# Second output projection as seven block products instead of eight, in a two-layer float32 transformer kernel on one Trainium2 core

## The chip, the cores and the metric

The kernel runs on one core of a Trainium2 chip. The metric is the device time of one execution in microseconds (us), as the median of three runs. TensorE (PE in the profile) multiplies, VectorE (DVE), ScalarE (ACT) and GpSimd (POOL) do the elementwise work, and SyncE (SP) issues most DMAs. Only VectorE and ScalarE read the PSUM banks that TensorE writes; GpSimd works in SBUF alone.

## The reference

Two transformer layers over a sequence of 512 tokens with model width 1024, all in float32. The first is an attention layer; the second is what matters here:

```
h = rms_norm(x, norm_mix);  proj = h @ w_in
a = nsa_attention(...) @ w_branch_attn        # 512 x 1024
b = pool_mixer(...) @ w_branch_pool           # 512 x 1024
ga, gb = split(sigmoid(g_merge))
x = x + (ga * a + gb * b) @ w_out             # the second output projection, 512 x 1024 by 1024 x 1024
h = rms_norm(x, norm_mlp)
x = x + square(relu(h @ w_ff1)) @ w_ff2       # feed forward, width 4096
return rms_norm(x, norm_final)
```

## The kernel before

Every matrix product is made from three: each operand is split into a high part (a copy by ScalarE into the type fp32r) and a low part (raw minus high, by VectorE or GpSimd), and `three` issues high x high, high x low and low x high into one PSUM bank. The program is one fixed instruction order per engine, written by hand, with counting semaphores between the engines; each engine takes its instructions strictly in that order.

Around the change the work runs so. In the branch stage TensorE makes 16 products of 12 matmuls each, in the order `BRANCH` (for column block e = 0 to 7 one for the pooled branch, n = 1, and one for attention, n = 0), round four banks. `branch_product` for e waits for `br_lo_done`, counted by `branch_low(e)` on VectorE, and for `r_free`, counted by `gate` of the product four earlier. VectorE multiplies each product with its gate (`gate`, L2610, one input in PSUM), adds the two (L2645, counted by `mix_done`, here called mix e), makes the low part of the branch weights two blocks ahead (`branch_low(e + 2)`, L2153), the low part of a unit of 1024 columns of the projection's weights (`w2o_lo`, L2652) and of the mixed activations (`m_lo`, L2655). ScalarE makes the high parts. GpSimd has nothing to do from 594.9 us, when its last attention work (`add_turned`) ends, to 690.8 us.

The second projection is `residual(R, ready2, product2, h3)`: for each of four row tiles i and two column halves n, eight chunks k of three matmuls with 512 columns. VectorE adds each bank to x (`add_x`, L2178, counted by `r_free`); when a row tile has both halves, ScalarE squares and sums it (`squares`), takes the root, and VectorE scales it (`norm`, L2111 and L2114). TensorE turns the normed tile (`h_transposes`, h3, L1015, eight 128 x 128 transposes) in the middle of the next tile's products, and VectorE and ScalarE make its high and low part (`take_halves`, L2166 and L2171, with `input_high` on ScalarE between). The first two feed-forward column tiles (`ff_tile`) are then made for the first three row tiles (384 columns), the last set of transposes between them, and then for the last row tile (128 columns):

```
for c in range(2):
    ff_tile(c, 0, 3 * P)
    if c == 0:
        h3(3)
pe.wait_ge(h_lo_done, halves("h3", NT - 1, 1) + 1)
for c in range(2):
    ff_tile(c, 3 * P, S).then_inc(a_full, 1)
```

The weights of the projection (`w2o0`, `w2o1`, one column half each) come by two DMAs issued before the branch stage. The first halves of w_ff1 (`f1_half`) are loaded by SyncE after the last branch product (two) and after the last use of `w2o0` (two); after `w2o1` follow the pairs of w_ff2. Behind the last h3 tile GpSimd makes sums of w_ff2 blocks (`pair_sums`), since the last product of the kernel already works with seven block products.

## Time and profile before

| | |
|---|---|
| median of 3 runs | 1022.66 us (1022.52 to 1022.76) |
| the profiled execution: its own time | 1021.85 us |
| its span, from the first to the last instruction | 1019.8 us |
| PE busy | 1006.5 us (99%) |
| VectorE busy | 680.1 us (67%) |
| ScalarE busy | 555.3 us (54%) |
| GpSimd busy | 418.7 us (41%) |
| granted TensorE clock | 1.00 over the span |

Times in the views are us from the span's start. In the windows' rows stand the stretch, its length, then for PE, PE's weight loads, VectorE, ScalarE and GpSimd the busy us with the number of instructions, the mean granted TensorE clock (1.00 is full), the DMA share and GB/s. In the timelines stand start, duration, engine, line, operation, output and inputs, shapes, how many instructions the row merges, and in brackets the idle time ahead of it with what ended it. Durations of matmuls overlap, so TensorE's rate is read from the starts.

### The profile page before, as it was taken

What the parts mean: (1) busy time and instruction counts of PE and PEld (TensorE: products, weight loads), DVE (VectorE), ACT (ScalarE), POOL (GpSimd) and SP (SyncE); (2) the same over time, 40 slices, a digit from 0 to 9 for tenths busy, and PEclk for the clock granted to TensorE, in tenths of its full rate; (3) what the DMA queues carried; (4) which work ended last, traced back from release to release, by engine and by line L of the source; (5) the groups of instructions that cost most, each with busy time, mean ns of one, the idle gap of its engine ahead of it and who ended that gap; (6) DMA issues with size and microseconds to landing.
All of it is one profiled execution on the core that took longest, in us unless ns stands there. A gap on an engine that the chain in (4) does not pass through costs nothing.

```text
span 1019.8 us, 14243 instructions
## 1 busy us (share of the span) xinstructions
PE 1006.5 (99%) x5158; PEld 828.2 (81%) x5158; DVE 680.1 (67%) x1201; ACT 555.3 (54%) x1013; POOL 418.7 (41%) x403
## 2 busy tenths in 40 slices
PE   9999999999999999999999999999999999999997
PEld 7788877778778898878887788888888888888886
DVE  5578898788984256733577889344222325999997
ACT  8455354777862456544667874224443446554555
POOL 0024012666720003900354520007769865875563
PEclk9999999999999999999999999999999999999999
DMA  9533321337140384132200453249999951443552
GB/s 339 105 98 97 100 62 42 84 84 196 53 175 1 123 284 129 45 100 63 63 2 1 149 166 100 83 136 308 353 343 333 340 208 62 155 137 143 207 186 83
DMA packets 100165, 146.24 MB, mean 143 GB/s; under 512 B 6480, under 2 KB 60496, under 8 KB 100096
## 3 DMA queue, kind: packets, MB, share of 16 engines
q1 hardware_dynamic: 86800, 130.75, 39.5%
q10 hardware_dynamic: 12768, 12.88, 4.1%
q0 software_dynamic: 528, 1.70, 0.9%
q8 instruction: 41, 0.67, 0.3%
q14 instruction: 28, 0.23, 0.1%
HBM read 123.69 MB, written 21.63 MB: 142 GB/s over the span
## 4 chain that ended last, share of the span: by engine, by line
PE 89%; DVE 6%; ACT 3%; issue 2%; POOL 0%; ACTq 0%; DVEq 0%; POOLq 0%
PE bank L966 60%; PE bank L1478 5%; PE bank L1479 5%; PE bank L1480 5%; PE bank L1358 2%; PE bank L1148 2%; PE bank L1367 2%; PE bank L1119 1%; DVE x L2244 1%; PE bank L1381 1%; DVE stats L2243 1%; DVE u_lo L2146 1%; PE bank L1132 1%; PE bank L1268 1%; PE bank L1015 1%
## 5 line engine op out<-in xcount | busy, mean ns | idle before, releaser
L2661 DVE TENSOR_TENSOR w_lo<-wring,w_hi 128x1024 fp32r<-128x1024 f32 x32 | 50.9, 1589 | 108.0 <-ACT w_hi L1999 108.0
L2146 DVE TENSOR_TENSOR u_lo<-wring,u_hi 128x1024 fp32r<-128x1024 f32 (+2 forms) x69 | 83.3, 1215 | 52.1 <-ACT u_hi L1652 51.6
L966 PE MATMUL bank<-u_hi,h_hi 128*128 128x512 f32 (+1 forms) x288 | 110.9, 385 | 0.1
L966 PE MATMUL bank<-u_hi,h_lo 128*128 128x512 f32 (+1 forms) x288 | 109.3, 379 | 0.0
L966 PE MATMUL bank<-u_lo,h_hi 128*128 128x512 f32 (+1 forms) x288 | 109.0, 378 | 0.0
L1652 ACT ACTIVATE u_hi<-wring 128x1024 fp32r<-128x1024 f32 (+1 forms) x64 | 66.0, 1033 | 69.3 <-PE bank L966 55.1
L966 PE MATMUL bank<-h_hi,w_hi 128*128 128x512 f32 (+2 forms) x272 | 103.2, 379 | 0.0
L966 PE MATMUL bank<-h_hi,w_lo 128*128 128x512 f32 (+2 forms) x272 | 103.1, 379 | 0.0
L966 PE MATMUL bank<-h_lo,w_hi 128*128 128x512 f32 (+2 forms) x272 | 103.1, 379 | 0.0
L966 PE MATMUL bank<-h_hi,u_hi 128*128 128x512 f32 x224 | 93.4, 417 | 0.4 <-ACT arena L1594 0.2
L966 PE MATMUL bank<-h_hi,u_lo 128*128 128x512 f32 x224 | 87.7, 392 | 0.0
L966 PE MATMUL bank<-h_lo,u_hi 128*128 128x512 f32 x224 | 87.6, 391 | 0.0
L1478 PE MATMUL bank<-s_hi,f_hi 128*128 128x512 f32 x224 | 87.3, 390 | 0.0
L1479 PE MATMUL bank<-s_hi,f_lo 128*128 128x512 f32 x224 | 87.2, 389 | 0.0
L1480 PE MATMUL bank<-s_lo,f_hi 128*128 128x512 f32 x224 | 87.2, 389 | 0.0
L1999 ACT ACTIVATE w_hi<-wring 128x1024 fp32r<-128x1024 f32 x32 | 33.9, 1060 | 91.9 <-PE bank L966 91.9
L2894 POOL TENSOR_SCALAR arena<-arena,stats 128x128 f32<-128x128 f32 (+3 forms) x64 | 40.6, 645 | 94.9 <-DVE stats L2617 94.8
L2687 DVE TENSOR_TENSOR s_lo<-wring,s_hi 128x2048 fp32r<-128x2048 f32 (+1 forms) x32 | 67.8, 2119 | 5.6 <-ACT s_hi L2029 5.6
L2840 POOL TENSOR_SCALAR x<-x,stats 128x128 f32<-128x128 f32 (+3 forms) x64 | 47.8, 753 | 55.4 <-DVE stats L2353 55.4
L966 PEld LDWEIGHTS bank<-u_hi,h_hi 128*128 128x128 f32 x288 | 54.1, 188 | 11.6 <-issue 1.2
L966 PEld LDWEIGHTS bank<-u_lo,h_hi 128*128 128x128 f32 x288 | 54.1, 188 | 10.3
L2029 ACT ACTIVATE s_hi<-wring 128x2048 fp32r<-128x2048 f32 (+1 forms) x32 | 54.3, 1696 | 14.0 <-PE bank L1480 13.8
(401 smaller groups left out, 2596.2 us busy)
## 6 DMA issues: line engine op xcount, KB each, us to landing
wring<-in_w_in SPq DMA_DIRECT2D x60, 512.0 KB, 3.9
wring<-in_w_ff ACTq DMA_DIRECT2D x12, 1024.0 KB, 9.4
wring<-sums_kept SPq DMA_DIRECT2D x16, 768.0 KB, 4.2
wring<-in_w_ff SPq DMA_DIRECT2D x22, 512.0 KB, 6.7
wring<-in_w_ff SPq DMA_DIRECT2D x32, 256.0 KB, 3.2
sums_kept<-wring SPq DMA_DIRECT2D x22, 256.0 KB, 4.9
wring<-in_w_out SPq DMA_DIRECT2D x2, 2048.0 KB, 12.7
wring<-in_w_ff SPq DMA_DIRECT2D x4, 1024.0 KB, 6.8
```

The costliest lines, as they stand in the source:

```text
L966: last = mm(b, lhs, rhs, start=(start and n == 0), stop=(stop and n == 2))
L1478: mm(b, f[0][:, token], w[0][:, high], start=start, stop=False)
L1479: mm(b, f[1][:, token], w[0][:, high], start=False, stop=False)
L1480: return mm(b, f[0][:, token], w[1][:, lows], start=False, stop=stop)
L1652: run(u_hi[hi_place(u)][:, 0:unit_cols(u)], raw_unit(u), ACT.Copy).then_inc(u_hi_done, 1)
L1999: run(dst, src, ACT.Copy).then_inc(w_hi_done, 1)
L2029: run(s_hi[m % 4][:, 0:PAIR - at], pair_raw(m)[:, at:PAIR], ACT.Copy).then_inc(s_hi_done, 1)
L2146: done = v.tensor_tensor(u_lo[raw_place(u)][:, cols], raw_unit(u)[:, cols], u_hi[hi_place(u)][:, cols].bitcast(F32), ALU.subtract)
L2661: v.tensor_tensor(cut(w_lo[ring3(m)]), src, cut(w_hi[ring3(m)]).bitcast(F32), ALU.subtract).then_inc(w_lo_done, 1)
L2687: v.tensor_tensor(s_lo[pair_place(m)][:, at:PAIR], pair_raw(m)[:, at:PAIR], s_hi[m % 4][:, 0:PAIR - at].bitcast(F32), ALU.subtract)
L2840: g.tensor_scalar(logits1[u % 8], logits1[u % 8], den[:, u:u + 1], unit_factor, ALU.mult, ALU.mult).then_inc(scaled, 1)
L2894: g.tensor_scalar(place, place, den2[:, u:u + 1], gates[:, i, at:at + 1], ALU.mult, ALU.mult).then_inc(scaled, 1)
```

## The change

The projection is cut into halves in all three dimensions: weights into quarters B11, B12, B21, B22 (512 x 512), activations into quarters of 256 tokens by 512. Eight block products become seven (B11, T2, T1, B22, B21, T3, T4 in this order, the list `seven`), with sums of weight quarters (T1 to T4) and of activation quarters (S1, S2, S4, and a difference in place in the lower half of m chunks 0 to 3). Each product is two row tiles t of four chunks. GpSimd makes the weight sums, three of 2048 columns per partition and one in two halves of 1024 (`quarter_sums`); VectorE the activation sums (`side_work`, three instructions of 256 columns for each of four chunks, and `last_side`, 1024 columns) and the low parts of quarters (`quarter_low`, two of 1024 columns each) and sides (`side_low`). Some of the fourteen results belong in two places of x; a running copy of B11 and T2, later with T3, in SBUF (`running`) is added to x by GpSimd, 512 columns six times (`add_running`). ScalarE makes the high parts of all of them and the first running copy. The h3 transposes move behind T3 (two sets) and into the first feed-forward tile (two sets), and the first two feed-forward tiles are made in halves of 256 columns. The unit high and low parts 0 and 1 of w_ff1 move ahead of the squares, and four buffers move. The loads of w_ff1 and w_ff2 wait for B21 and T3 in place of the projection's last products.

```diff
+        seven = ("B11", "T2", "T1", "B22", "B21", "T3", "T4")
...
+        HIGHS = ("B11", "B22", "T1", "T2", "B21", "T3", "T4")
+        QUARTER_SUM_ORDER = ("T1", "T3", "T2", "T4")
+        QUARTER_READ_BY = {"B11": "T1", "T1": "T2", "B22": "T2", "T2": "T4", "B21": "T4"}
+        high_count = lambda name, h: 2 * HIGHS.index(name) + h + 1
+        low_count = lambda name, h: 2 * seven.index(name) + h + 1
...
+        out2_bank = {"B11": 2, "T2": 6, "T1": 0, "B22": 4, "B21": 2, "T3": 6, "T4": 6}
+        def out2_used(name):
+            return R_OUT2 + 2 * seven.index(name) + 2
+        def out2_added(i):
+            return R_OUT2 + (2 * seven.index("B21") + i if i < 2 else 2 * seven.index("T4") + i - 2) + 1
...
+            out2_sides = {"B11": (m_hi[0:4], m_lo[0:4], 0), "B21": (m_hi[4:8], m_lo[4:8], 0), "T3": (m_hi[0:4], m_lo[0:4], 2 * P),
+                          "T4": (m_hi[4:8], m_lo[4:8], 2 * P), "T2": "S2", "T1": "S1", "B22": "S4"}
+            out2_behind = {"B11": R_OUT2 - 1, "B21": out2_used("T2") - 1, "T3": out2_used("T2") - 1, "T4": out2_used("T3") - 1}
+            def out2(name, t):
+                if name in out2_behind:
+                    pe.wait_ge(r_free, out2_behind[name] + t)
+                q = seven.index(name)
+                for j in range(4):
+                    if t == 0 and j % 2 == 0:
+                        pe.wait_ge(w2o_lo_done, low_count(name, j // 2))
+                    if isinstance(out2_sides[name], str):
+                        if t == 0 and j == 0:
+                            pe.wait_ge(side_lows, SIDE_LOWS + ("S2", "S1", "S4").index(out2_sides[name]) + 1)
+                        side = side_hi[out2_sides[name]], side_lo[out2_sides[name]]
+                        rows = slice((2 * j + t) * P, (2 * j + t + 1) * P)
+                    else:
+                        highs, lows, at = out2_sides[name]
+                        if t == 0 and name in ("B11", "B21"):
+                            pe.wait_ge(m_lo_done, (0 if name == "B11" else 4) + j + 1)
+                        side = highs[j], lows[j]
+                        rows = slice(at + t * P, at + (t + 1) * P)
+                    last = three(bank[out2_bank[name] + t][:, :], (w2o_hi[q % 4], w2o_lo[name, j // 2]), slice(512 * j, 512 * (j + 1)), side, rows,
+                                 False, j == 0, j == 3, j % 2 * 512)
+                last.then_inc(r_full, 1)
...
-            residual(R, ready2, product2, h3)
-            R += 2 * NT
-            def ff_tile(c, first, end):
-                for k in range(KC):
+            def ff_tile(c, first, end, chunks=range(KC)):
+                for k in chunks:
                     last = three(bank[AT[("ff", c)] % 2][:, first:end], (w_hi[ring3(c)], w_lo[ring3(c)]), slice(k * P, (k + 1) * P),
                                  (h_hi, h3_lo), slice(k * S + first, k * S + end), True, k == 0, k == KC - 1)
                 return last
...
+            for name in seven:
+                for t in range(2):
+                    out2(name, t)
+                    if name == "T3":
+                        h3(t)
+            pe.wait_ge(r_free, out2_used("B21"))
+            pe.wait_ge(h_lo_done, halves("h3", 1, 1) + 1)
+            a_bank(("ff", 0))
+            pe.wait_ge(w_lo_done, 1)
+            ff_tile(0, 0, 2 * P, range(3))
+            h3(2)
+            ff_tile(0, 0, 2 * P, range(3, KC))
+            h3(3)
+            a_bank(("ff", 1))
+            pe.wait_ge(w_lo_done, 2)
+            ff_tile(1, 0, 2 * P)
             pe.wait_ge(h_lo_done, halves("h3", NT - 1, 1) + 1)
             for c in range(2):
-                ff_tile(c, 3 * P, S).then_inc(a_full, 1)
-            pe.wait_ge(r_free, R)
+                ff_tile(c, 2 * P, S).then_inc(a_full, 1)
+            pe.wait_ge(r_free, out2_added(NT - 1))
...
+            def quarter_high(name, h):
+                q = seven.index(name)
+                if name == "B11":
+                    arrived(act, "w2o0")
+                elif name == "B22":
+                    arrived(act, "w2o1")
+                elif name in QUARTER_SUM_ORDER:
+                    act.wait_ge(quarter_sums, QUARTER_SUMS + QUARTER_SUM_ORDER.index(name) + 1)
+                if q >= 4:
+                    act.wait_ge(r_full, out2_used(seven[q - 4]))
+                run(w2o_hi[q % 4][:, D * h:D * (h + 1)], w2o_raw[name, h], ACT.Copy).then_inc(w2o_hi_done, 1)
+            def side_high(name):
+                act.wait_ge(r_full, R_OUT2)
+                act.wait_ge(side_sums, SIDE_SUMS + (13 if name == "S4" else 12))
+                run(side_hi[name][:, :], side_raw[name], ACT.Copy).then_inc(side_highs, 1)
+            EARLY_HIGHS = [(name, h) for name in HIGHS[0:4] for h in range(2)]
             for e in range(KC):
-                n, c = e // 4, slice(UNIT * (e % 4), UNIT * (e % 4 + 1))
-                if e % 4 == 0:
-                    arrived(act, f"w2o{n}")
-                run(w2o_hi[n][:, c], wring[:, SLOT * n:SLOT * (n + 1)][:, c], ACT.Copy).then_inc(w2o_hi_done, 1)
+                quarter_high(*EARLY_HIGHS[e])
                 if 1 <= e < KC - 2:
                     branch_high(e + 2)
-                act.wait_ge(mix_done, e + 1)
-                run(m_hi[e][:, :], gaT[:, e, :], ACT.Copy).then_inc(m_hi_done, 1)
+                if e >= 4:
+                    act.wait_ge(mix_done, e + 1)
+                    run(m_hi[e][:, :], gaT[:, e, :], ACT.Copy).then_inc(m_hi_done, 1)
+                    act.wait_ge(side_sums, SIDE_SUMS + 3 * (e - 4) + 2)
+                    run(m_hi[e - 4][:, :], gaT[:, e - 4, :], ACT.Copy).then_inc(m_hi_done, 1)
+            def copy_first(t):
+                act.wait_ge(r_free, R_OUT2 + t + 1)
+                run(running[t], bank[out2_bank["B11"] + t][:, :], ACT.Copy).then_inc(first_copied, 1)
+            side_high("S2")
+            side_high("S1")
+            copy_first(0)
+            side_high("S4")
+            copy_first(1)
+            for name in ("B21", "T3", "T4"):
+                for h in range(2):
+                    quarter_high(name, h)
...
-            for i in range(NT):
-                if i >= 1:
-                    input_high("h3", i - 1)
-                squares(2 * NT, R_OUT2, i)
-                if i in (1, 2):
-                    unit_hi(i - 1)
-            input_high("h3", NT - 1)
+            unit_hi(0)
+            unit_hi(1)
+            nc.scalar.preload_act_table(ACT.Sqrt)
+            for i in range(2):
+                squares(2 * NT, out2_added(i), i)
+            for i in range(2):
+                input_high("h3", i)
+            for i in range(2, NT):
+                squares(2 * NT, out2_added(i), i)
             unit_hi(2)
...
+            def quarter_low(name, h):
+                dve.wait_ge(w2o_hi_done, high_count(name, h))
+                if name in QUARTER_READ_BY:
+                    dve.wait_ge(quarter_sums, QUARTER_SUMS + QUARTER_SUM_ORDER.index(QUARTER_READ_BY[name]) + 1)
+                q = seven.index(name)
+                v.tensor_tensor(w2o_lo[name, h][:, :], w2o_raw[name, h], w2o_hi[q % 4][:, D * h:D * (h + 1)].bitcast(F32), ALU.subtract)\
+                    .then_inc(w2o_lo_done, 1)
+            def mixed2_low(k):
+                dve.wait_ge(m_hi_done, 2 * k + 2 if k < 4 else 2 * k - 7)
+                dve.wait_ge(side_sums, SIDE_SUMS + (3 * k + 3 if k < 4 else 13))
+                v.tensor_tensor(m_lo[k][:, :], gaT[:, k, :], m_hi[k][:, :].bitcast(F32), ALU.subtract).then_inc(m_lo_done, 1)
+            def side_work(j):
+                upper, lower, other = gaT[:, j, 0:2 * P], gaT[:, j, 2 * P:S], gaT[:, j + 4, 2 * P:S]
+                s1, s2 = side_part(side_raw["S1"], j), side_part(side_raw["S2"], j)
+                dve.wait_ge(mix_done, j + 5)
+                v.tensor_tensor(s1, lower, other, ALU.add).then_inc(side_sums, 1)
+                v.tensor_tensor(lower, upper, lower, ALU.subtract).then_inc(side_sums, 1)
+                dve.wait_ge(side_sums, SIDE_SUMS + 3 * j + 1)
+                v.tensor_tensor(s2, s1, upper, ALU.subtract).then_inc(side_sums, 1)
+                mixed2_low(j)
+            def last_side():
+                dve.wait_ge(r_full, R_OUT2)
+                dve.wait_ge(side_sums, SIDE_SUMS + 12)
+                by_chunk = lambda a: a.rearrange("p (j s) -> p j s", j=4)
+                v.tensor_tensor(by_chunk(side_raw["S4"]), gaT[:, 4:8, 0:2 * P], by_chunk(side_raw["S2"]), ALU.subtract).then_inc(side_sums, 1)
+            def side_low(n, name):
+                dve.wait_ge(side_highs, SIDE_HIGHS + n + 1)
+                if name == "S2":
+                    dve.wait_ge(side_sums, SIDE_SUMS + 13)
+                v.tensor_tensor(side_lo[name][:, :], side_raw[name], side_hi[name][:, :].bitcast(F32), ALU.subtract).then_inc(side_lows, 1)
+            def out2_add(name, t):
+                part = bank[out2_bank[name] + t][:, :]
+                dve.wait_ge(r_full, R_OUT2 + 2 * seven.index(name) + t + 1)
+                xs = lambda i, n: x[:, i, n * 512:(n + 1) * 512]
+                if name == "T2":
+                    dve.wait_ge(first_copied, FIRST_COPIED + t + 1)
+                elif name == "T3":
+                    dve.wait_ge(running_added, RUNNING_ADDED + t + 1)
+                elif name == "T1":
+                    v.tensor_tensor(xs(2 + t, 1), xs(2 + t, 1), part, ALU.add)
+                    dve.wait_ge(running_added, RUNNING_ADDED + t + 1)
+                elif name == "B22":
+                    dve.wait_ge(r_free, out2_used("T1") - 1 + t)
+                elif name == "B21":
+                    dve.wait_ge(r_free, out2_used("B11") - 1 + t)
+                elif name == "T4":
+                    dve.wait_ge(running_added, RUNNING_ADDED + 2 * t + 3)
+                place = {"B11": xs(t, 0), "T2": running[t], "T1": xs(t, 1), "B22": xs(t, 1), "B21": xs(t, 0), "T3": running[t], "T4": xs(2 + t, 0)}[name]
+                v.tensor_tensor(place, place, part, ALU.add).then_inc(r_free, 1)
+            LOW_AT = {3: (("B11", 0), ("B11", 1)), 6: (("T2", 0),), 7: (("T2", 1), ("T1", 0))}
...
-                n, c = e // 4, slice(UNIT * (e % 4), UNIT * (e % 4 + 1))
-                dve.wait_ge(w2o_hi_done, e + 1)
-                v.tensor_tensor(w2o_lo[n][:, c], wring[:, SLOT * n:SLOT * (n + 1)][:, c], w2o_hi[n][:, c].bitcast(F32), ALU.subtract)\
-                    .then_inc(w2o_lo_done, 1)
-                dve.wait_ge(m_hi_done, e + 1)
-                v.tensor_tensor(m_lo[e][:, :], gaT[:, e, :], m_hi[e][:, :].bitcast(F32), ALU.subtract).then_inc(m_lo_done, 1)
+                if e >= 4:
+                    side_work(e - 4)
+                for name, h in LOW_AT.get(e, ()):
+                    quarter_low(name, h)
...
+            last_side()
+            side_low(0, "S2")
             dve.wait_ge(x_back, 16 * NT)
...
+            out2_add("B11", 0)
+            side_low(1, "S1")
+            quarter_low("T1", 1)
+            out2_add("B11", 1)
+            quarter_low("B22", 0)
+            quarter_low("B22", 1)
+            out2_add("T2", 0)
+            side_low(2, "S4")
+            mixed2_low(4)
+            out2_add("T2", 1)
+            mixed2_low(5)
+            mixed2_low(6)
+            out2_add("T1", 0)
+            mixed2_low(7)
+            quarter_low("B21", 0)
+            out2_add("T1", 1)
+            quarter_low("B21", 1)
+            quarter_low("T3", 0)
+            out2_add("B22", 0)
+            quarter_low("T3", 1)
+            quarter_low("T4", 0)
+            out2_add("B22", 1)
+            quarter_low("T4", 1)
+            unit_lo(0)
+            out2_add("B21", 0)
+            unit_lo(1)
+            out2_add("B21", 1)
+            norm(2 * NT, 0, xn3)
+            norm(2 * NT, 1, xn3)
+            out2_add("T3", 0)
+            take_halves("h3", 0, V_G3, h3_lo)
+            out2_add("T3", 1)
+            take_halves("h3", 1, V_G3, h3_lo)
+            out2_add("T4", 0)
+            norm(2 * NT, 2, xn3)
+            out2_add("T4", 1)
+            take_halves("h3", 2, V_G3, h3_lo)
+            norm(2 * NT, 3, xn3)
+            take_halves("h3", 3, V_G3, h3_lo)
...
+            raw_quarter = lambda n, h: wring[:, SLOT * n + QUARTER * h:SLOT * n + QUARTER * (h + 1)]
+            t1_raw, t2_raw = (region_of[place][:, at:at + QUARTER] for place, at in (quarter_at["T1"], quarter_at["T2"]))
+            arrived(pool, "w2o0")
+            arrived(pool, "w2o1")
+            pool.wait_ge(last_lo_done, 2)
+            g.tensor_tensor(t1_raw, raw_quarter(1, 0), raw_quarter(0, 0), ALU.subtract).then_inc(quarter_sums, 1)
+            g.tensor_tensor(raw_quarter(1, 0), raw_quarter(1, 1), raw_quarter(1, 0), ALU.subtract).then_inc(quarter_sums, 1)
+            pool.wait_ge(mix_done, 4)
+            pool.wait_ge(quarter_sums, QUARTER_SUMS + 1)
+            g.tensor_tensor(t2_raw, raw_quarter(1, 1), t1_raw, ALU.subtract).then_inc(quarter_sums, 1)
+            pool.wait_ge(quarter_sums, QUARTER_SUMS + 3)
+            for h in range(2):
+                part = slice(D * h, D * (h + 1))
+                done = g.tensor_tensor(w2o_raw["T4", h], raw_quarter(0, 1)[:, part], t2_raw[:, part], ALU.subtract)
+            done.then_inc(quarter_sums, 1)
+            def add_running(i, n, t):
+                xs = x[:, i, n * 512:(n + 1) * 512]
+                g.tensor_tensor(xs, xs, running[t], ALU.add).then_inc(running_added, 1)
+            pool.wait_ge(x_back, 16 * NT)
+            for t in range(2):
+                pool.wait_ge(r_free, out2_used("T2") - 1 + t)
+                add_running(t, 1, t)
+            for t in range(2):
+                pool.wait_ge(r_free, out2_used("T3") - 1 + t)
+                add_running(2 + t, 0, t)
+                add_running(2 + t, 1, t)
```

## Rows read from the trace of the kernel before

**Rows 1.** The page, part 1: busy time and share of the span of each engine.
```profile
PE 1006.5 (99%) x5158; PEld 828.2 (81%) x5158; DVE 680.1 (67%) x1201; ACT 555.3 (54%) x1013; POOL 418.7 (41%) x403
```

**Rows 2.** Windows: branch stage, then second projection.
```profile
602.50:636.94 34.44, 34.44 (x153) 28.52 (x152) 31.62 (x41) 16.17 (x19) 0.00 (x0) 1.00 0.45 138
636.94:683.17 46.23, 46.23 (x217) 38.52 (x216) 20.61 (x31) 11.85 (x19) 0.00 (x0) 1.00 0.25 80
```

**Rows 3.** Timeline of PE: start, duration, line, operation, shapes.
```profile
634.22 0.39 PE L966 MATMUL bank<-a_hi,br_hi 128*128 128x512 f32 x1
...
636.94 0.39 PE L966 MATMUL bank<-w2o_hi,m_hi 128*128 128x512 f32 x1
...
683.17 0.33 PE L966 MATMUL bank<-h_hi,w_hi 128*128 128x384 f32 x1
...
687.36 1.03 PE L1015 MATMUL bank<-consts,arena 128*128 128x128 f32 x8
...
688.15 0.42 PE L966 MATMUL bank<-h_hi,w_hi 128*128 128x384 f32 x1
...
692.41 0.22 PE L966 MATMUL bank<-h_hi,w_hi 128*128 128x128 f32 x1
...
697.71 0.45 PE L966 MATMUL bank<-h_hi,w_hi 128*128 128x512 f32 x1
```

**Rows 4.** Timeline of PE, matmuls of 256 columns, four starts apart.
```profile
593.69 0.28 PE L1381 MATMUL bank<-pt_hi,v_both 128*128 128x256 f32 x1
...
594.16 0.28 PE L1381 MATMUL bank<-pt_hi,v_both 128*128 128x256 f32 x1
```

**Rows 5.** Timeline of VectorE at the head of the branch stage.
```profile
600.97 0.42 DVE L2589 TENSOR_TENSOR a_lo<-arena,a_hi 128x256 fp32r<-128x256 f32 x1 [0.48 <-ACT a_hi L1927]
601.31 1.22 DVE L2153 TENSOR_TENSOR br_lo<-wring,br_hi 128x1024 fp32r<-128x1024 f32 x1
602.45 1.38 DVE L2610 TENSOR_TENSOR arena<-arena,bank 128x512 f32<-128x512 f32 x2
603.86 0.69 DVE L2645 TENSOR_TENSOR arena<-arena 128x512 f32<-128x512 f32 x1
...
605.61 0.68 DVE L2655 TENSOR_TENSOR m_lo<-arena,m_hi 128x512 fp32r<-128x512 f32 x1
606.21 0.68 DVE L2610 TENSOR_TENSOR arena<-arena,bank 128x512 f32<-128x512 f32 x1
```

**Rows 6.** Timeline of GpSimd, adds and subtractions with two inputs in SBUF.
```profile
271.47 0.74 POOL L2822 TENSOR_TENSOR junk<-arena,x 128x256 f32<-128x256 f32 x1
...
585.22 1.31 POOL L2905 TENSOR_TENSOR br_lo<-wring,br_hi 128x512 fp32r<-128x512 f32 x1
...
690.83 1.29 POOL L2919 TENSOR_TENSOR wring<-wring 128x512 f32<-128x512 f32 x1 [95.94 <-DVE h_lo L2171]
692.08 2.26 POOL L2920 TENSOR_TENSOR wring<-wring 128x512 f32<-128x512 f32 x1
...
883.11 2.49 POOL L2938 TENSOR_TENSOR arena<-arena 128x256 f32<-128x256 f32 x1 [1.20 <-PE bank L1480]
```

**Rows 7.** Timeline of VectorE at the same moments.
```profile
585.68 0.69 DVE L2599 CUSTOM_DVE_ANT_0 arena<-bank,consts 128x512 f32<-128x512 f32 x1 [0.25 <-PE bank L1358]
...
691.00 2.20 DVE L2661 TENSOR_TENSOR w_lo<-wring,w_hi 128x1024 fp32r<-128x1024 f32 x1 [0.25 <-ACT w_hi L1999]
...
882.72 2.28 DVE L2687 TENSOR_TENSOR s_lo<-wring,s_hi 128x2048 fp32r<-128x2048 f32 x1
```

**Rows 8.** Timeline of VectorE, from a bank add to the norm behind it.
```profile
659.79 0.69 DVE L2178 TENSOR_TENSOR x<-x,bank 128x512 f32<-128x512 f32 x1 [3.05 <-PE bank L966]
...
662.09 0.16 DVE L2111 RECIPROCAL stats<-stats 128x1 f32<-128x1 f32 x1 [1.60 <-ACT stats L1539]
662.28 0.76 DVE L2114 TENSOR_SCALAR arena<-x,stats 128x1024 f32<-128x1024 f32 x1
```

**Rows 9.** Windows: behind the last matmul.
```profile
1014.00:1019.80 5.80, 0.00 (x0) 0.00 (x0) 1.55 (x3) 1.97 (x5) 0.00 (x0) 0.94 0.66 248
```

More of the change, by code:

```diff
@@ L499, in wo_high_of @@
             return zb_half[:, k:k + count, :] if k < 4 else qk1_half[:, 1, (k - 4) // 2:(k - 4) // 2 + 1, (K_LO, OUTS)[k % 2], :]
[L501 to L504 removed]
+        QUARTER, SIDE = SLOT // 2, D
@@ L1856, in _ @@
             high(U2)
[L1857 removed]
+            squares(NT, 2, 0)
             for u in range(1, HI_UNITS - 1):
```

107 lines of the change are left out of this document (58 added, 49 removed).

## The prediction

> **What bounds the kernel now.** The page comes first: PE is busy 99% of the span [rows 1]. TensorE sets the time, so a change is worth the PE time it removes minus the PE idle time it makes. The windows cut the place into the branch stage and the second output projection; PE idles in neither, and VectorE is busy 31.6 of 34.4 us in the first and 20.6 of 46.2 us in the second [rows 2]. The reader should note that VectorE is nearly full just where GpSimd is about to get work. The PE timeline gives the pitches and the marks: the last branch product starts at 634.22 and the projection at 636.94, so a matmul of 512 columns has a pitch of 2.72 / 12 = 0.227 us; the first feed-forward tiles run from 683.17 to 697.71 [rows 3].
>
> **What is removed.** The projection has 4 row tiles x 2 column halves x 8 chunks x 3 = 192 matmuls, and seven products have 7 x 2 row tiles x 4 chunks x 3 = 168: 24 x 0.227 = 5.4 us. The first feed-forward tiles now cost 4.19 + 4.26 us at 384 columns and 5.30 us at 128, 13.75 us without the transposes [rows 3]. At 256 columns the pitch is (594.16 - 593.69) / 4 = 0.1175 us [rows 4], so 96 of them take 11.3 us, 2.5 us less. Gross gain 7.9 us; the stretch from 636.94 to 697.71 (60.8 us) would be 52.9 us if PE never waited.
>
> **Durations.** VectorE, both inputs in SBUF: 0.34 us from start to start at 256 columns, 0.60 at 512, 1.14 at 1024; with one input in PSUM 0.60 at 512 [rows 5]. GpSimd, two inputs: 0.74 us at 256 and 1.29 at 512 [rows 6]. No row has 2048 columns. A straight line through these two gives 4.6 us, four times 1.29 gives 5.2; I take 4.6 and keep 5.2 for the range. For 1024 it is 2.4 us.
>
> **How the two engines share.** The view to read is the timelines of GpSimd and VectorE side by side. The 1024 subtraction at 691.00 finds the GpSimd add of 690.83 running: it takes 2.20 us in place of 1.22, which is waiting to about 692.1 and then its own time; and the add of 692.08 takes 2.26 in place of 1.29, having waited for that subtraction. At 883.11 a 256 add takes 2.49 us behind the 2048 subtraction of 882.72, which ends at 885.0. An operation with a PSUM input is not held (585.68, 0.69 us inside the add of 585.22) [rows 6, 7]. So whole instructions exclude each other, the waiting engine goes next, and I take it that a 4.6 us add shuts VectorE out for 4.6 us. The row for such a length is VectorE's (2.2 us), not GpSimd's. The Trainium skill (SBUF — State Buffer, on the shared GPSIMD/Vector port) has the same rule: an exclusive lock held for the full instruction, not a split of bandwidth; it speaks against this change, and the rows agree with it up to 2.2 us. The skill (GPSIMD Engine Reference, section 3.1) gives 4.5 us for a 2048 float32 add; by that the sum below would be about 0.3 us lower.
>
> **Branch stage, step by step.** The last of the sixteen products (p = 15) starts at 634.22 [rows 3], so product p starts at 634.22 - 2.72 (15 - p). Product 2e needs branch_low(e), which VectorE issues behind mix(e - 2); a product also needs the gate of four earlier. GpSimd's first sum is ready when last_low(1) ends (601.4), waits for the branch_low of 601.31 and runs 602.5 to 607.1. Gates 1 and 2 (PSUM) pass; mix 0, issued at 603.86 now [rows 5], waits to 607.1. The second sum takes the port at 607.7, when mix 0 ends, to 612.2. Gate 3 passes; mix 1 runs 612.2 to 612.8, branch_low(3) to 614.0. Product 6, due at 609.74, starts at 614.1: PE waits 4.4 us. Without sums VectorE catches up until mix 3 (621.1) and branch_low(5) (622.2). The third sum holds the port 622.2 to 626.8, the low part of B11,0 follows to 627.9, then the fourth sum in two halves with B11,1 between them to 633.75; mix 4 ends at 634.35, branch_low(6) at 635.5. Product 12, after the first shift due at 630.4, starts at 635.6: 5.2 us more. These two waits come from the length of one GpSimd instruction; sums of 5.2 us make them 12 us together. From there VectorE keeps pace and the last branch product ends at 646.5, 9.6 us late.
>
> **Between the stages.** Before, m_lo of chunk 7 was due 5 us into the first product. Now B11's fourth chunk is due after 2.0 us (9 matmuls), and stands behind gate 15, mix 7, three side operations of 256 columns, ScalarE's high part and a low part, on VectorE also behind the low part of T2,0. From mix 6 on that is worked out as 651.5 against 648.5: 3.0 us. T2 then waits for the low parts T2,1 and T1,0, the 1024 side S4 and the low part of S2, 4 x 1.14 us, while PE has 3.4 us of B11 left: 1.2 us. T2 starts at 656.1.
>
> **Inside the projection.** From T2's start VectorE has, up to B21's second add: two side, nine quarter and two unit low parts of 1024 columns (13 x 1.14), four m_lo and twelve bank adds (16 x 0.60), 24.4 us, and two running adds of GpSimd that shut it out for 1.3 us each. By this queue B21,0 is added at 25.2 us, though PE had it at 19.0. From an add to the reciprocal of its norm pass 2.30 us [rows 8], and norm 0 is ready at 27.9; PE, done with T3,0 at 24.5, waits for it: 3.4 us. Four more running adds fall on the low parts of take_halves 0 and 1, and the feed-forward start waits 0.5 us for h_lo. norm 2 (add of T4,0 at 39.0, plus the squares) is ready at 41.6 when PE wants it at 39.5: 2.1 us. norm 3 stands behind take_halves 2; from the start of a set of transposes to the last low part behind it are 691.00 - 0.25 - 687.36 = 3.4 us [rows 3, 7], then 0.95 us for reciprocal and norm [rows 8]: PE waits 1.8 us at the last transposes. The stretch from T2's start to the end of the first tiles takes 47.7 + 7.8 = 55.5 us.
>
> **What I cost at nothing.** ScalarE's added copies (four running and side highs, m_hi, quarters): it is busy 16.2 of 34.4 and 11.9 of 46.2 us [rows 2]. GpSimd's own time: it is idle in both stretches, and its weight sums of the next stage start after the last h_lo as before. The DMAs of w_ff1 wait for B21 and T3 in place of the end of the projection, earlier relative to it; if they were late, unit_hi(4) would be next. The Sqrt table load moves ahead of the squares.
>
> **Sum.** Waits 4.4 + 5.2 + 3.0 + 1.2 + 7.8 = 21.6 us against 7.9 us: +13.7 us, on the profiled execution's 1021.85 us (span 1019.8) 1035.6; the median of the runs shown is 0.8 us above that execution, so 1036.4 us.
>
> **Rivals.** (a) Long sums don't hold the port throughout, short ones do: branch_low(3) and (6) come in time, 9.6 us fall away, +4 us, 1027. For it: no row shows a GpSimd hold beyond 1.3 us. Against it: those of 1.3 us are undivided. (b) The port costs nothing here at all: VectorE's queue alone is left, waits 2.5 + 1.2 between the stages and 2.9 inside, 6.6 against 7.9: -1.3 us, 1021.4. Against it stands 691.00. (c) Faster: VectorE's queue is not late inside and between the stages (operations overlap more than my pitches, or ready marks come earlier) and the sums fall into its gaps: only the removed matmuls count, up to -7.9, 1014.8. It decides once all waits together are under 5.8 us; the stage before was 92% full on VectorE, which speaks against it. (d) The clock falls in the long waits. The only fall in this trace is behind the last matmul, with PE idle from 1014 on: a mean of 0.94 over 5.8 us is a level of one half for the last 0.7 us, so it fell after some 5 us of idling [rows 9], and the second wait is 5.2 us. One product at 1.2 GHz in place of 2.4 costs 2.7 us: +3 to +6 on top, 1040 to 1043. The Trainium skill (TensorE: Matmul & The Clock Gate, HAM oscillation) says that an idle gap of this order halves the clock; by that the time would be 1040.
>
> **Chances.** The forecast with (d) as its upper part, +9 to +20: 0.65 (0.5 without a clock fall, 0.15 with). (a), +2 to +9: 0.16. (b): 0.09. (c): 0.08. Above 1043: 0.02. 0.2% is 2.0 us, about what a measurement of this kernel tells from no change. Faster 0.09, same 0.09, slower 0.82. Range 1025 to 1043: its lower end is (a) less 2 us, its upper one the sums of 5.2 us (+2.4) or two clock falls.
>
> **What would show it.** Right: the GpSimd rows of the sums near 4.6 us; mix 0 and mix 1 on VectorE of 4 to 5 us; PE idle ahead of products 6 and 12, 4 to 5 us each; PE idle ahead of B11's fourth chunk and of three sets of h3 transposes; VectorE without gaps from B11 to B21. Wrong: PE busy 34.4 us over the branch stage (then (a) or (b)), or VectorE waiting for PE inside the projection (then (c)); a granted clock under 1.00 beside these waits is (d).

## The result, and the profile after

The changed kernel takes 1042.43 us (median of 4 runs, 1040.19 to 1042.70) against 1022.67 (4 runs, 1022.52 to 1022.76) for the kernel before: ratio 1.0187, 95% interval 1.0171 to 1.0203. The forecast was 1036.4 in a range of 1025 to 1043. The page of the kernel after, its busy times and the rows of its 40 slices for PE, VectorE, GpSimd and the granted clock, then the shares of the chain:

```profile
span 1040.9 us, 14292 instructions
PE 1009.3 (97%) x5134; PEld 827.9 (80%) x5134; DVE 716.8 (69%) x1231; ACT 565.3 (54%) x1024; POOL 451.4 (43%) x414
PE   9999999999999999999999988888999999999997
DVE  5578997789984349435577878984222325999997
POOL 0024012667610006500554544126669974875553
PEclk9999999999999999999999988999999999999999
PE 81%; DVE 11%; ACT 4%; issue 3%; POOL 0%; ACTq 0%; DVEq 0%; POOLq 0%
```

PE was 99% busy [rows 1]; it now has five slices with gaps, and they are the slices from the branch products to the first feed-forward tiles. The same view by windows, the branch stage to the start of block B11 and from there to the first full feed-forward tile, answers to [rows 2]:

```profile
602.50:651.43 48.93, 40.57 (x153) 32.38 (x152) 40.47 (x40) 14.49 (x18) 21.51 (x5) 0.86 0.32 97
651.43:718.79 67.36, 57.55 (x298) 48.91 (x296) 56.37 (x71) 28.51 (x41) 17.39 (x11) 0.95 0.39 129
```

The reader should see three things. Both stretches grew: 34.4 to 48.9, and 60.8 to 67.4 though fewer matmuls stand in it. VectorE is busy 56.4 us of the second. And the granted clock is under 1 in both (0.86, 0.95), where it was 1.00. The PE timeline shows each wait as the idle time in brackets, with what ended it:

```profile
613.68 0.80 PE L1016 MATMUL bank<-pm_hi,br_hi 128*128 128x512 f32 x1 [3.81 <-DVE br_lo L2264]
...
637.65 0.80 PE L1016 MATMUL bank<-pm_hi,br_hi 128*128 128x512 f32 x1 [4.54 <-DVE br_lo L2264]
...
656.36 0.50 PE L1016 MATMUL bank<-w2o_hi,m_hi 128*128 128x512 f32 x1 [2.73 <-DVE m_lo L2766]
...
688.50 1.09 PE L1065 MATMUL bank<-consts,arena 128*128 128x128 f32 x8 [2.25 <-DVE arena L2225]
...
701.90 1.09 PE L1065 MATMUL bank<-consts,arena 128*128 128x128 f32 x8 [1.79 <-DVE arena L2225]
...
707.71 1.35 PE L1065 MATMUL bank<-consts,arena 128*128 128x128 f32 x8 [2.93 <-DVE arena L2225]
```

These are product 6, product 12, B11's fourth chunk, and the transposes of input tiles 0, 2 and 3. GpSimd and VectorE side by side in the branch stage:

```profile
601.52 5.44 POOL L3112 TENSOR_TENSOR arena<-wring 128x2048 f32<-128x2048 f32 x1 [6.67 <-DVE a_lo L2701]
606.92 5.02 POOL L3113 TENSOR_TENSOR wring<-wring 128x2048 f32<-128x2048 f32 x1
623.75 5.53 POOL L3116 TENSOR_TENSOR arena<-wring,arena 128x2048 f32<-128x2048 f32 x1 [11.82 <-DVE arena L2814]
```

```profile
603.83 3.68 DVE L2814 TENSOR_TENSOR arena<-arena 128x512 f32<-128x512 f32 x1
607.43 0.67 DVE L2722 TENSOR_TENSOR arena<-arena,bank 128x512 f32<-128x512 f32 x1
608.14 4.35 DVE L2814 TENSOR_TENSOR arena<-arena 128x512 f32<-128x512 f32 x1
612.41 1.21 DVE L2264 TENSOR_TENSOR br_lo<-wring,br_hi 128x1024 fp32r<-128x1024 f32 x1
...
625.59 8.11 DVE L2760 TENSOR_TENSOR w2o_lo_B<-wring,w2o_hi 128x1024 fp32r<-128x1024 f32 x2
```

Mixings 0 and 1 take 3.68 and 4.35 us in place of 0.69; the gate between them reads PSUM and is not held, also inside a GpSimd sum. Behind mixing 1 stands branch_low(3), which product 6 needs. Last, the windows of the granted clock (the number before the last two) around product 6:

```profile
612.00:614.00 2.00, 0.32 (x1) 0.32 (x2) 2.00 (x3) 1.07 (x2) 0.00 (x0) 0.71 1.06 320
614.00:616.00 2.00, 2.00 (x6) 1.52 (x6) 1.97 (x4) 1.98 (x2) 0.00 (x0) 0.50 0.29 119
616.00:618.00 2.00, 2.00 (x6) 1.62 (x5) 0.68 (x1) 0.02 (x1) 0.00 (x0) 0.50 0.00 0
618.00:620.00 2.00, 2.00 (x7) 1.53 (x7) 0.69 (x1) 0.00 (x0) 0.00 (x0) 0.59 0.00 0
620.00:625.00 5.00, 5.00 (x23) 4.12 (x22) 2.53 (x4) 0.00 (x0) 1.25 (x1) 1.00 0.30 84
```

The clock drops to 0.50 (1.2 GHz of 2.4) in the wait and product 6 then runs 5.29 us instead of 2.72.

### The profile page after: what moved, and what is told of

Its sections match the earlier page's. It is cut to its first block, busy times and chain, and to the rows that moved or that the text cites. A ratio compares the mean times of both kernels' runs of the same rounds, so it can differ in the third digit from the quotient of the medians.

```text
span 1040.9 us, 14292 instructions
## 1 busy us (share of the span) xinstructions
PE 1009.3 (97%) x5134; PEld 827.9 (80%) x5134; DVE 716.8 (69%) x1231; ACT 565.3 (54%) x1024; POOL 451.4 (43%) x414
## 4 chain that ended last, share of the span: by engine, by line
PE 81%; DVE 11%; ACT 4%; issue 3%; POOL 0%; ACTq 0%; DVEq 0%; POOLq 0%
PE bank L1016 52%; PE bank L1550 5%; PE bank L1552 5%; PE bank L1551 5%; PE bank L1408 2%; PE bank L1198 2%; PE bank L1417 2%; PE bank L1169 1%; DVE x L2356 1%; PE bank L1431 1%; DVE stats L2355 1%; DVE u_lo L2257 1%; PE bank L1182 1%; DVE w2o_lo_B L2760 1%; DVE w2o_lo_T L2760 1%
## 5 line engine op out<-in xcount | busy, mean ns | idle before, releaser
L1016 PE MATMUL bank<-h_hi,w_hi 128*128 128x512 f32 (+1 forms) x272 | 103.4, 380 | 0.1
L1016 PE MATMUL bank<-h_lo,w_hi 128*128 128x512 f32 (+1 forms) x272 | 103.0, 379 | 0.0
L1016 PE MATMUL bank<-h_hi,w_lo 128*128 128x512 f32 (+1 forms) x272 | 102.9, 378 | 0.0
L2140 ACT ACTIVATE s_hi<-wring 128x2048 fp32r<-128x2048 f32 (+1 forms) x32 | 54.3, 1696 | 13.8 <-PE bank L1552 13.6
```

Source lines behind the costliest of these rows:

```text
L1016: last = mm(b, lhs, rhs, start=(start and n == 0), stop=(stop and n == 2))
L2140: run(s_hi[m % 4][:, 0:PAIR - at], pair_raw(m)[:, at:PAIR], ACT.Copy).then_inc(s_hi_done, 1)
```

## The experiments

Two stretches on the PE timeline give a common measure for all of them: A, from the last 256-column matmul ahead of the branch stage (near 597) to B11's first matmul (in kernels without blocks, the projection's first), and B, from there to the first full feed-forward tile. Read so, the change made A 14.5 us longer (39.9 to 54.5) and B 6.6 us (60.8 to 67.4, against the 52.9 that the prediction gives for no wait).

| kernel | A, us | B, us | time, us | ratio to before (95%) |
|---|---|---|---|---|
| before | 39.9 | 60.8 | 1022.5 to 1022.9 | |
| after | 54.5 | 67.4 | 1042.43 | 1.0187 (1.0171 to 1.0203) |
| e1: sums in pieces of 512 | 45.1 | 68.4 | 1032.33 | 1.0089 (1.0072 to 1.0107) |
| e2: no sums | 40.1 | 65.8 | 1027.58 | 1.0046 (1.0031 to 1.0061) |
| e3: filler matmuls | 50.6 | 67.4 | 1038.28 | 1.0148 (1.0132 to 1.0164) |
| e4: before + halves | 40.0 | 59.3 | 1020.98 | 0.9982 (0.9973 to 0.9991) |
| e5: order behind B22 | 52.3 | 63.0 | 1037.20 | 1.0151 (1.0135 to 1.0166)|
| e6: pieces, all orders | 43.1 | 64.8 | 1028.92 | 1.0063 (1.0050 to 1.0076) |
| e7: sums on VectorE | 41.5 | 69.2 | 1031.31 | 1.0083 (1.0069 to 1.0097) |
| e8: before + two long sums | 48.2 | 60.8 | 1030.95 | 1.0084 (1.0069 to 1.0099) |
| e9: e7 with orders | 40.8 | 65.9 | 1027.96 | 1.0054 (1.0039 to 1.0069) |
| e10: orders, no sums | 40.0 | 64.1 | 1025.56 | 1.0028 (1.0017 to 1.0039) |

**e1, the sums in pieces.**

```
+def weight_quarter_sum(out, left, right, columns=QUARTER, piece=512):
+    for at in range(0, columns, piece): ... g.tensor_tensor(out[:, part], left[:, part], right[:, part], ...)
-g.tensor_tensor(t1_raw, raw_quarter(1, 0), raw_quarter(0, 0), ALU.subtract)
+weight_quarter_sum(t1_raw, raw_quarter(1, 0), raw_quarter(0, 0))     # the same for the others
```

> The changed kernel with each weight sum cut into pieces of 512 columns (16 GpSimd instructions in place of 5), nothing left out. Theory (the length of one GpSimd instruction is what delays branch_low): no wait of VectorE for the port is longer than 1.3 us, the wait ahead of product 6 falls from 4.0 us to under 1, the one ahead of product 12 from 4.7 to 1 to 3 us because about 10 us of exclusion are still laid on a full VectorE, and neither wait brings the clock down: 1029 to 1034 us. Rival (it is the amount of GpSimd work, not its length): both waits stay about as long, 1039 to 1043 us.

Measured 1032.33. Not one column less is added, and the time falls by 10.1 us: most of what the sums cost is the length of one instruction. VectorE's instructions of the branch stage take 13.8 us more than their own time beside the long sums and 9.8 us more beside the pieces, so both engines still pay. GpSimd's first two sums and VectorE's first instructions beside them:

```profile
601.29 6.79 POOL L3115 TENSOR_TENSOR arena<-wring 128x512 f32<-128x512 f32 x4 [6.67 <-DVE a_lo L2701]
608.04 7.47 POOL L3115 TENSOR_TENSOR wring<-wring 128x512 f32<-128x512 f32 x4
```

```profile
603.59 1.62 DVE L2814 TENSOR_TENSOR arena<-arena 128x512 f32<-128x512 f32 x1
605.14 0.67 DVE L2722 TENSOR_TENSOR arena<-arena,bank 128x512 f32<-128x512 f32 x1
605.84 1.07 DVE L2814 TENSOR_TENSOR arena<-arena 128x512 f32<-128x512 f32 x1
```

The mixings now take 1.62 and 1.07 us, a piece 1.7 to 1.9 instead of 1.29 [rows 6]: the engines take turns. Product 6 no longer waits; product 12 still waits 2.7 us, and there the expectation failed: the clock fell behind that wait too, to 0.50 for 3.4 us, and twice more at the transposes of tiles 0 and 3.

**e2, no sums.** The weight sums are left out: GpSimd memsets of the same places stand for them, so the weights of T1 to T4 are constants and the output is not the reference's.

```
-g.tensor_tensor(t1_raw, raw_quarter(1, 0), raw_quarter(0, 0), ALU.subtract).then_inc(quarter_sums, 1)
+g.memset(t1_raw, 1.0).then_inc(quarter_sums, 1)        # the same for the others
```

> The changed kernel with the weight sums left out: GpSimd fills their places with memsets, which write SBUF and read nothing, so the second projection is computed with wrong weights. Theory: the waits ahead of products 6 and 12 and the two falls of the clock behind them are gone, 8.7 + 5.8 us, of which 1 to 2 come back as the wait ahead of T2 that the slow clock had hidden: 1029 to 1031 us. What is left over the kernel before is VectorE's queue in the projection. Rival (VectorE's own added work delays branch_low): still a wait of some us ahead of product 12, over 1034 us. If a memset excludes VectorE as a sum does, its rows are shorter (2 us) and so are VectorE's waits.

Measured 1027.58, 1.4 us under the expected stretch and still slower than before. A is back at 40.1: the whole lateness of the branch stage, clock included, was the sums'. Without them the kernel is 14.9 us faster than the changed one: the 10.1 us of their length (e1) and 4.8 us of their amount. B is 65.8, 13 us over its waitless 52.9. T2's wait for its low parts, hidden in the changed kernel, shows here with 1.1 us. One row pair surprised:

```profile
604.13 1.82 POOL L3113 MEMSET wring<- 128x2048 f32 x1
```

```profile
604.73 0.69 DVE L2814 TENSOR_TENSOR arena<-arena 128x512 f32<-128x512 f32 x1
```

The mixing runs inside a memset of 2048 columns and takes its normal 0.69 us: this GpSimd instruction, which only writes, does not hold VectorE. The later memsets show the same: a low part of 1024 columns takes its 1.22 us beside them.

**e3, filler matmuls for the clock.**

```
 e, n = BRANCH[at]
+if at in (6, 12):
+    pe.wait_ge(r_free, 2 * NT + at - 3)
+    for _ in range(12):
+        mm(bank[6][:, :], a_hi[:, 0:P], a_hi[:, 0:S], start=True, stop=True)     # read by nobody
 pe.wait_ge(br_lo_done, e + 2)
```

> The changed kernel with 12 added matmuls of 512 columns into an unused bank ahead of the waits of products 6 and 12 each; they fill 2.7 us of waits of 4.0 and 4.7 us and change no result. Theory (the clock falls because PE idles, and costs on top of the waits): no fall at these two places, the products behind take 2.7 us in place of 5.3 and 3.1, 1036 to 1038 us, since 1 us may come back ahead of T2. Rival (the time behind the waits is VectorE's, the slow products are hidden by it): 1041 to 1043 us.

Measured 1038.28, 4.15 us less than after, just above the theory's stretch. Twelve matmuls are 2.7 us of work; they shortened the idle time at product 6 to 1.15 us and the clock stayed at 1.00 there. At product 12 1.87 us were left and the clock still fell (0.66 over 635 to 640), against the expectation. Added work on the waiting engine made the kernel faster: the slow clock is a cost of its own.

**e4, the halves alone, on the kernel before.**

```
-    ff_tile(c, 0, 3 * P)
+    ff_tile(c, 0, 2 * P)
...
-    ff_tile(c, 3 * P, S).then_inc(a_full, 1)
+    ff_tile(c, 2 * P, S).then_inc(a_full, 1)
```

> The kernel before with one part alone: the first two feed-forward tiles in halves of 256 columns instead of 384 and 128, the last transposes between them. 96 matmuls of 0.1175 us in place of 13.75 us: 2.5 us less on PE. The first half tile is 1.4 us shorter than the tile of 384 columns, so the last transposes come 1.4 us earlier and wait for norm 3 by 0.1 to 0.8 us, and the last low parts may come 0.5 us late. Theory: 1.2 to 2.4 us faster, 1020.3 to 1021.5 us. Rival (the earlier transposes wait as long as the halves save): 1022 to 1023 us.

Measured 1020.98, faster than before, and the only kernel of this study that is. On its PE timeline, 24 matmuls run from 684.00 to the transposes, 72 after them (the first full tile starts at 697.06):

```profile
684.00 0.28 PE L966 MATMUL bank<-h_hi,w_hi 128*128 128x256 f32 x1
...
687.50 1.09 PE L1015 MATMUL bank<-consts,arena 128*128 128x128 f32 x8 [0.47 <-DVE arena L2114]
688.35 0.36 PE L966 MATMUL bank<-h_hi,w_hi 128*128 128x256 f32 x1
```

Without the wait of 0.47 that is 3.0 + 8.7 = 11.7 us against 13.75: the halves give 2.0 us, and a new wait of half a microsecond: counted from the projection's first matmul, TensorE is ready for the transposes of tile 3 after 49.3 us in place of 50.4, and they start after 49.7.

**e5, the order of two queues.**

```
-quarter_low("T4", 1); unit_lo(0); out2_add("B21", 0); unit_lo(1); out2_add("B21", 1)
-norm(2 * NT, 0, xn3); norm(2 * NT, 1, xn3)
+out2_add("B21", 0); quarter_low("T4", 1); norm(2 * NT, 0, xn3)
+out2_add("B21", 1); unit_lo(0); norm(2 * NT, 1, xn3); unit_lo(1)
...
-take_halves("h3", 2, V_G3, h3_lo); norm(2 * NT, 3, xn3)
+take_halves("h3", 2, V_G3, h3_lo, between=norm 3)      # and ScalarE: unit_hi(2) behind input_high("h3", 2)
```

> The changed kernel, long sums and all, with one thing altered: the order of VectorE's and ScalarE's queues behind product B22. The adds of B21 and norms 0 and 1 stand ahead of the last T4 low and of the two feed-forward lows, norm 3 stands between the products and the lows of input transpose 2, and ScalarE's high of the third feed-forward tile goes behind input high 2. Theory (the waits ahead of the transposes of tiles 0 and 3 are queueing: VectorE had work of later use in front of the adds and the norms): the waits of 2.4 and 3.2 us fall under 0.6 us each, and the fall of the clock behind the second, 1.6 us, goes with them, so the time falls by 4 to 7 us, to 1035 to 1038.5. Rival (the waits are the chain itself, from the last matmul over add, squares, root and norm to the transpose): the time moves by less than 1 us, 1041.5 to 1042.5.

Measured 1037.20, 5.2 us less. The 2.3 us ahead of the transposes of tile 0 are gone, those of tile 3 wait 0.26 in place of 2.93, and the clock no longer falls there. So both were queueing. What came instead is 1.24 us at the second row tile of T4 (its bank is free only after T3's second add, which stands behind the low parts of input 0) and 0.7 at the first feed-forward matmul; tile 2's 1.8 us stayed, being the chain of add, squares, root and norm itself.

**e6, pieces and all orders together.** e1 and e5, and:

```
-LOW_AT = {3: (("B11", 0), ("B11", 1)), 6: (("T2", 0),), 7: (("T2", 1), ("T1", 0))}
+LOW_AT = {5: (("B11", 0), ("B11", 1)), 6: (("T2", 0),)}        # T2,1 behind side_low S2, T1,0 behind side_low S1
+for chunks in (range(3), range(3, 4)):                          # TensorE: B11 by chunks, both row tiles
+    for t in range(2):
+        out2("B11", t, chunks)
-ff_tile(0, 0, 2 * P, range(3))
+ff_tile(0, 0, 2 * P, range(5))
```

> The kernel with the sums in pieces of 512 columns (1032.3 us) with the order of the run beside it, and with four more moves: the lows of block B11 behind mixing 5 instead of 3, the lows of T2's second half and of T1 behind the low of side sum S2, the products of B11's first three chunks for both row tiles ahead of the fourth chunk of either, and the transposes of tile 2 behind five chunks of the first feed-forward tile instead of three. Theory (what is left over the gross gain is queueing in front of five waits, and the clock that falls in them): of the 12.6 us of waits in the pieces' trace 9 to 11 go (2.7 ahead of product 12, 2.2 of 3.8 around B11 and T2, 5 of 5.9 at the norms) and about 3 us of slow clock, so 1018.5 to 1022.5, on a par with the kernel before or faster. Rival (the waits move to other places, since VectorE is full while GpSimd adds): 1026 to 1031.

Measured 1028.92: the theory's 1018.5 to 1022.5 was wrong, and the rival right. The clock stays at 1.00 from the branch stage on, but instead of e1's seven waits there are thirteen, 10.9 us in all, none over 1.6 us, and all but one ended by VectorE. The waits moved. A short wait also costs more than its idle time: in e2, B11's ninth matmul starts at 639.75 and the next at 642.86, which is 0.15 us more than the pitch of 0.23 and the idle 2.73, and the two starts behind it come 0.12 us late; about 0.27 us for each restart. The other waits between matmuls of 512 columns in e6, e9 and e10 show the same 0.24 to 0.29 us, where the idle time is half a microsecond or more.

**e7, the sums on VectorE**, T1's behind mixing 0, T3's behind 2, T2's behind 3 and T4's halves behind 4 and 5:

```
+def weight_sum(at): ... v.tensor_tensor(t1_raw, raw_quarter(1, 0), raw_quarter(0, 0), ALU.subtract).then_inc(quarter_sums, 1) ...
+    weight_sum(e)                        # in VectorE's loop over the mixings; GpSimd's five sums taken out
```

> The changed kernel with the five weight sums on VectorE, behind mixings 0, 2, 3, 4 and 5, in place of GpSimd. Theory (the delay came from VectorE standing still while a long GpSimd sum ran, 17.8 us in all, though the sums are worth about 9.4 us of VectorE's own time): with the sums in VectorE's own queue the stage is as late as with the pieces, 1029 to 1036. Rival (what made the stage late is the amount of added work, wherever it stands): 1040 or more.

Measured 1031.31, 11.1 us less than with the sums on GpSimd. A is 41.5, better than with pieces on GpSimd (45.1). In its own queue the five sums are 9.3 us of VectorE's time, about the 9.8 us that the pieces on GpSimd hold it up. (The 17.8 us of the expectation are the sums' own time on GpSimd; VectorE stood still for 13.8 of them.) The offload to GpSimd bought nothing even in its mild form.

**e8, two long sums in the kernel before**, and nothing else of the change. The result is read by nobody; the two waits were over long before.

```
+for n in range(2):
+    g.tensor_tensor(arena[:, 25728:27776], wring[:, SLOT:SLOT + 2048], wring[:, SLOT + 2048:2 * SLOT], ALU.subtract)
+act.wait_ge(pooled, len(POOL_WINDOWS) + 2)     # ahead of m_hi 6; VectorE the same ahead of w2o low 4
```

> The kernel before, nothing of the change in it, with two GpSimd subtractions of 2048 columns (from the raw second output weights into an unused stretch of the arena, the result read by nobody) at the place where the changed kernel has its first two sums. Theory (VectorE stands still while a long GpSimd sum runs, and is the engine that the block products wait for): VectorE loses about 8.7 us of which the stage has 2.8 us idle, one block product waits 4 to 6 us, and the clock falls behind it for another 2.5 to 3.4 us: 1028 to 1032. Rival (the sums delay nothing by themselves; the changed kernel is late by the work that it adds to VectorE's own queue): 1022 to 1024.

Measured 1030.95, 8.4 us more than before. GpSimd, VectorE, PE and the clock of its trace:

```profile
602.08 10.44 POOL L2916 TENSOR_TENSOR arena<-wring 128x2048 f32<-128x2048 f32 x2 [6.64 <-issue]
```

```profile
604.42 3.68 DVE L2647 TENSOR_TENSOR arena<-arena 128x512 f32<-128x512 f32 x1
608.02 5.59 DVE L2656 TENSOR_TENSOR w2o_lo<-wring,w2o_hi 128x1024 fp32r<-128x1024 f32 x1
```

```profile
616.73 0.80 PE L966 MATMUL bank<-pm_hi,br_hi 128*128 128x512 f32 x1 [6.27 <-DVE br_lo L2155]
```

```profile
612.00:614.00 2.00, 0.00 (x0) 0.00 (x0) 2.00 (x2) 0.00 (x0) 0.53 (x1) 0.87 1.12 314
614.00:616.00 2.00, 0.00 (x0) 0.00 (x0) 1.97 (x4) 0.43 (x1) 0.00 (x0) 0.50 0.76 278
616.00:618.00 2.00, 1.27 (x3) 1.09 (x4) 2.00 (x3) 2.00 (x3) 0.00 (x0) 0.50 0.00 0
```

Mixing 0 takes 3.68 us as in the changed kernel, the low part behind it 5.59 instead of 1.22, product 6 waits 6.3 us, a little over the expected 4 to 6, and then runs at half clock. A grows by 8.25 us and B by nothing. This separates the mechanism from everything else in the change.

**e9, e7 with the orders of e6** (B11's lows behind mixings 5 and 6, T2's first behind the last mixing).

> The weight sums on VectorE (1031.3 us) together with the reordered queues (1028.9 us with the sums in pieces on GpSimd), block B11's two lows one behind each of mixings 5 and 6, and T2's first low behind the last mixing. Theory (VectorE has more to do from the branch products to the feed-forward than TensorE, so an order shifts the waits but can't take them away, and where the sums stand is worth little): 1025 to 1029, slower than before. Rival (the waits left are the fault of single misplaced instructions): 1018 to 1022.5.

Measured 1027.96, as the theory said; ten waits, 10.1 us.

**e10, those orders without any sums**: e9 with the memsets of e2.

> The reordered queues of the run beside it, with the weight sums left out of both engines: GpSimd memsets stand in their place, so the weights of T1, T2, T3 and T4 are constants and the output is not the reference's. It shows the time of seven products if their weight sums cost nothing. Theory (beside the sums the change gives VectorE side sums, more lows and more adds, which alone use up the gross gain of 7.9 us): 1021 to 1025, no faster than before. Rival (only the sums stood in the way of the gain): 1015 to 1018.

Measured 1025.56, just above the theory's stretch and slower than before by 0.28% (0.17 to 0.39). If the weight sums cost nothing, and the orders are mended, seven products still lose. The windows say why, the branch stage and the stretch behind it:

```profile
603.40:637.90 34.50, 34.50 (x154) 28.55 (x153) 25.98 (x40) 14.62 (x18) 6.15 (x5) 1.00 0.43 137
637.90:703.00 65.10, 57.04 (x302) 46.72 (x301) 56.91 (x72) 29.12 (x42) 17.54 (x11) 1.00 0.40 130
```

In the second stretch VectorE is busy 56.9 us. In the kernel before it was 20.6 of the first 46.2 [rows 2] and 28.4 of all 60.8. As the queues stand, seven products need 52.9 us of TensorE and about 57 us of VectorE there; so VectorE is the longer one, even with no gap. The windows of e10 from B11's first matmul to about the first of the feed-forward (685.97), and then stretch A of e10 and of the kernel before:

```profile
637.74:686.40 48.66, 42.66 (x189) 32.95 (x187) 46.90 (x57) 20.12 (x27) 10.57 (x6) 1.00 0.40 130
```

```profile
597.79:637.74 39.95, 39.91 (x177) 32.71 (x176) 30.48 (x48) 19.54 (x24) 7.23 (x5) 1.00 0.38 119
```

```profile
597.02:636.94 39.92, 39.88 (x177) 32.71 (x176) 36.16 (x49) 20.50 (x25) 0.00 (x0) 1.00 0.39 119
```

VectorE is busy 46.9 of 48.7 us (96%) where TensorE waits for it. But it is idle for 9.5 us of A, where the kernel before had 3.8: that kernel made seven of its eight low parts of projection weights in A, e10 makes one of fourteen there. Over A and B together VectorE has 87.6 us of work in e10 (64.5 before), and TensorE needs 92.8. So full is VectorE behind the branch stage in this order, and not over both stages; whether low parts moved forward, B22's for instance, would take the waits away, no run shows.

## Why the prediction was right or wrong

**Right: the sums.** The length was taken as 4.6 us; GpSimd's records are 5.44, 5.02 and 5.53 with the wait for VectorE in them; from the end of the VectorE instruction that each waited for they are 4.4 to 4.5 us. VectorE stood still for 3.0 and 3.7 us (3.68 and 4.35 less 0.69). Rival (a), long sums don't hold, and (b), nothing does, fell with these rows, with e1 and with e8. The rule cited from the Trainium skill (SBUF — State Buffer, Who interferes with whom) holds here for sums of 2048 columns, 1.3 us being the longest hold seen before. The same section limits it, for a VectorE instruction with two inputs in SBUF, to a GpSimd instruction that reads SBUF, not one that only writes; the memset of e2 agrees (0.69 us for the mixing inside it).

**Right: the places and sizes of the waits**, counted by the starts of the matmuls, so with their restart. Product 6: 4.4 forecast, 3.98 measured. Product 12: 5.2, 4.71. B11's fourth chunk: 3.0, 2.88. Transposes 0: 3.4, 2.41. Feed-forward start: 0.5, 0.27. Transposes 2: 2.1, 1.95. Transposes 3: 1.8, 3.09; this one was undersized: ScalarE's unit_hi(2) stands ahead of input high 2, which the prediction didn't count. e5 moved it, and norm 3 as well, and the wait was gone. T2's start: 1.2 forecast, none seen, because the slow clock stretched B11 until T2's parts were ready (e2, with no fall there, shows 1.1). Sum 21.6 forecast, 19.3 measured.

**Nearly right: the gross gain.** 7.9 us forecast; 24 matmuls of 0.227 us stand, and the halves gave 2.0 us in place of 2.5 (e4), because the pitch of 256 columns is 0.12 us there and not 0.1175, and the restarts behind the transposes cost. So 7.4. (The prediction's 47.7 us of PE work from T2's start should be 47.5, 52.9 less B11's 5.4; its sum doesn't use the figure.)

**Wrong: the clock's share.** The forecast of 1036.4 left the clock at full speed and gave its fall, rival (d), 0.15. It fell four times: at products 6 and 12, in B11, and behind the transposes of tile 3. By matmul starts that is 2.6 + 2.6 us, 0.4 + 0.4 in the products behind them, 1.7 and 1.6: 9.2 us before rounding. The step that failed is "it fell after some 5 us of idling [rows 9], and the second wait is 5.2 us": one fall behind the last matmul was read as the length of idle time that it takes, and only the second wait was held to be long enough. The falls came with waits of 3.8 us (product 6), 2.7 us (B11) and 2.9 us (transposes 3) too. The accounts close: -7.4 + 19.3 + 9.2 = +21.1 us, as between the two profiled spans (1040.9 and 1019.8). By the Trainium skill (TensorE: Matmul & The Clock Gate, HAM oscillation) the prediction estimated 1040, which is nearer; the trace agrees with the page that waits of a few microseconds can halve the clock, and e3 shows that filling them helps.

That 1042.43 lies inside the range, 0.6 us below its end, is in part luck. The clock cost 9.2 us where (d) allowed 3 to 6, and the waits came out 2.3 us smaller than forecast; had they come as forecast, the time would have been above 1043.

**What the sum didn't say.** The prediction treats the waits inside the projection as matters of queue order (and two were, e5). e6, e9 and e10 show what stands behind most of them: VectorE has more work there than the seven products give TensorE time. That is why e6's expectation asked too much of orders inside the projection. That no order at all would mend it is not shown: in the branch stage VectorE has room (e10). B of e10, 64.1 us, is 52.9 + 8.1 of idle time + 3.1; nine restarts of 0.27 and the 0.5 us that the halves give less make 2.9 of it.

## What to carry to other kernels

Before giving work to GpSimd beside a VectorE that is nearly full, compare both sides as one engine: a sum with two inputs in SBUF cost VectorE about what it cost in its own queue (9.8 us in e1, 9.3 in e7), and undivided it also cost the wait behind one long hold (e8); cut it into short instructions or leave it on VectorE. When a matrix product is replaced by fewer products and more sums, add up the sums' engine over the same stretch first: 5.4 us of matmuls were saved here and VectorE's work in the stretch doubled (28.4 to 57.1 us in e10, while that of the branch stage fell by 5.7). Give the fall of the clock a price and a chance at every TensorE wait of some microseconds: in the traces here it came with 16 of the 19 waits of 2.4 us and more and with 1 of the 10 between 1.7 and 2.3 us, and cost about 1.5 to 3 us of slow matmuls each time.
